# Norm chain moved to the end of the stage that makes the tokens, in a two-block transformer kernel on one core

## The chip, the core and the metric

One Trainium2 chip, one of its cores. The metric is the device time of one execution in microseconds, from the first to the last instruction of the program and what lies around it. All arithmetic is fp32 or, for the large products, pairs of fp32r parts.

## The reference

Two stacks of two layers each on 256 latent tokens of width 1024 (the first stack also carries 256 context tokens, so 512 in all, until its last mixer). Every layer is

```python
x = x + 0.5 * ffn(rms_norm(x, g1))          # SwiGLU, 1024 -> 2 x 2816 -> 1024
x = x + mixer(rms_norm(x, g2))              # attentions, a convolution, a product out
x = x + 0.5 * ffn(rms_norm(x, g3))

def rms_norm_2(x, g, eps=NORM_EPS):
    xf = x.astype(jnp.float32)
    y = xf * lax.rsqrt(jnp.mean(xf * xf, axis=-1, keepdims=True) + eps)
    return (y * g.astype(jnp.float32)).astype(x.dtype)
```

(in the first stack with a gate, a gain and a shift made from a conditioning vector). A last norm follows. That makes 13 norms: 5 on 512 tokens and 8 on 256.

## The kernel before, in words

Tokens are kept transposed: `k.x` is [128, 8, tokens], features on partitions in 8 chunks, tokens along the row. The program is a sequence of stages: `conditioning` (product `mod0`), then for each layer `half_ffn`, a mixer behind `norm_tokens`, `add_product_of_parts` (product `out`), `half_ffn`, and at the end `norm_tokens` and `ending`. Each stage is one or more `Block`s. Within a block each engine runs its own list of instructions in the order written, and a block ends when all engines have reached its end.

All weights come through a ring of 4 slots (`RING`), one unit of up to 128 x 2048 at a time, loaded by SP as PE finishes with a slot (`unit_done`). Before PE uses a unit it is split in two fp32r parts: ACT copies it to the high part (`split_high`, L472), then DVE subtracts to get the low part (`split_low`, L480). PE takes three matmuls for each product of parts (L496). Part buffers are 2 deep in stages on 512 tokens and in the mixers, 4 deep in `half_ffn` on 256 tokens.

The norm has two ends. Where a stage makes new tokens, ACT squares each chunk of `k.x` (L390) and POOL adds the squares of chunks 0 to 6 (L405); the last square stays apart. Where the next stage begins, PE sums both over the partitions with a matrix of ones (L418, L420), which leaves in PSUM the sum of squares of each token, equal on all 128 partitions; ACT takes the root of it (L967 or L513), DVE the reciprocal into `k.rinv` (L1053 or L537), and both of them go over 128 x tokens elements. `half_ffn` then scales chunk by chunk on DVE (L1060), shifts or copies on ACT to the high part `normed[0]` (L974, L976), and DVE makes the low part `normed[1]` (L1072, L1074); PE's first unit of the stage takes the chunks as they come. In `norm_tokens` the scaling is L544 or L541, and the block ends before the mixer's first matmul.

In `half_ffn`, ACT's list begins with the split of unit 0, the root, the split of unit 1, and then the 8 chunks; DVE's with the low part of unit 0, the reciprocal, then the chunks, then the low part of unit 1:

```python
            split_high(act, 0, 0)
...
            nc.scalar.activation(k.root[:, T], k.psum[:, 0, T], ACT.Sqrt, bias=k.eps[:, 0:1], scale=1.0 / D)\
                .then_inc(t["root_done"].sem, 1)
            split_high(act, 0, 1)
```

In `hybrid_mixer` (the mixer of the second stack) the norm's block splits unit 0 of the mixer's first product in the same way, so that `project_heads` begins with unit 0 ready. `conditioning` multiplies the conditioning vector with 9 units, places the results, and squares the opening tokens.

## Time and profile before

| | |
|---|---|
| time, median of 3 executions | 3957.33 us (3955.28 to 3962.86) |
| the profiled execution: its own time | 3963.74 us |
| its span, first to last instruction | 3961.7 us |
| PE busy with matmuls | 3490.9 us (88% of the span) |
| DVE, ACT, POOL busy | 2099.9 us (53%), 1412.2 us (36%), 229.1 us (6%) |
| mean granted TensorE clock | 0.933 of 2.4 GHz |

The profiled execution is 6.4 us longer than the median. A busy share is an average over all stages. For this change what counts is the stretch between one stage's last matmul and the next stage's first ones, 13 of them, and who is waited for there.

### The profile page before, as it was taken

The page shows a single profiled execution, that of the slowest core. Times are in us where ns is not written, and L with a number is a line of the kernel's source. Part 1 is how long each engine was busy: PE and PEld are TensorE (multiplying, and loading weights), DVE is VectorE, ACT ScalarE, POOL GpSimd, SP SyncE. Part 2 cuts the span into 40 slices and gives each one's busy share as a digit, 9 for nine tenths or more (in the row PEclk, how much of TensorE's full clock was granted, in tenths as well). Part 3 has the DMA queues.
Part 4 walks back from the last instruction along what each step waited for, and adds up shares of the span by engine and source line. Part 5 has one row for each costly group of instructions (what it writes and reads, how often), then busy time and mean ns, then how long its engine had stood idle before and what let it go on. Part 6 is the DMA issues. An engine that isn't in the chain of part 4 may idle for free. (4 is left out here: it accounts for less than half of the span.)

```text
span 3961.7 us, 54085 instructions
## 1 busy us (share of the span) xinstructions
PE 3490.9 (88%) x20506; PEld 2972.5 (75%) x20506; DVE 2099.9 (53%) x2729; ACT 1412.2 (36%) x2278; POOL 229.1 (6%) x169
## 2 busy tenths in 40 slices
PE   5999896789998999898799998769899999769898
PEld 4887642468887788664699998548899999548898
DVE  5767474547677433214454655554455545554554
ACT  3323302233333322212444544243344444243443
POOL 0000100100001000200000001200000001200000
PEclk8999898889999999998899999879999999879899
DMA  6666420016665233320166565204466564104464
GB/s 200 184 180 178 110 62 31 0 59 168 186 175 157 82 96 94 101 96 0 43 175 176 150 188 155 56 0 112 141 171 180 163 188 145 53 1 126 127 185 133
DMA packets 766417, 478.33 MB, mean 121 GB/s; under 512 B 35093, under 2 KB 743173, under 8 KB 766101
## 3 DMA queue, kind: packets, MB, share of 16 engines
q1 hardware_dynamic: 755872, 473.14, 42.2%
q10 hardware_dynamic: 10356, 2.63, 0.4%
q8 instruction: 126, 2.06, 0.2%
q14 instruction: 63, 0.51, 0.0%
HBM read 474.65 MB, written 1.05 MB: 120 GB/s over the span
## 5 line engine op out<-in xcount | busy, mean ns | idle before, releaser
L496 PE MATMUL psum<-normed,weights_part 128*128 128x256 f32 (+1 forms) x11232 | 1738.4, 317 | 86.7 <-DVE normed L1074 27.3
L496 PEld LDWEIGHTS psum<-normed,weights_part 128*128 128x128 f32 x11232 | 1586.7, 192 | 227.3 <-issue 82.1
L480 DVE TENSOR_TENSOR weights_part<-weights,weights_part 128x2048 fp32r<-128x2048 f32 (+1 forms) x397 | 847.4, 2137 | 755.3 <-ACT weights_part L472 755.1
L472 ACT ACTIVATE weights_part<-weights 128x2048 fp32r<-128x2048 f32 (+1 forms) x397 | 708.4, 1787 | 761.7 <-PE psum L496 350.1
L496 PE MATMUL psum<-hidden,weights_part 128*128 128x256 f32 (+1 forms) x4224 | 680.7, 323 | 0.0
L496 PEld LDWEIGHTS psum<-hidden,weights_part 128*128 128x128 f32 x4224 | 614.5, 190 | 61.5
L1267 DVE SCALAR_TENSOR_TENSOR stage<-weights,cond,stage 128x768 f32<-128x768 f32 x294 | 281.1, 1019 | 0.0
L405 POOL TENSOR_TENSOR square<-square,rinvs 128x256 f32<-128x256 f32 (+1 forms) x39 | 57.2, 1466 | 2490.3 <-ACT rinvs L390 2488.2
L1101 DVE SCALAR_TENSOR_TENSOR x<-psum,gate,x 128x256 f32<-128x256 f32 (+1 forms) x112 | 49.6, 479 | 130.8 <-PE psum L496 130.8
L858 DVE TENSOR_REDUCE negmax<-psum 128x1 f32<-128x256 f32 (+1 forms) x128 | 66.8, 524 | 94.7 <-PE psum L2347 20.0
L987 ACT ACTIVATE rinvs<-psum 128x256 f32<-128x256 f32 (+1 forms) x88 | 39.9, 453 | 212.9 <-PE psum L496 212.8
L1524 PE MATMUL psum<-h,weights 128*128 128x512 f32 (+1 forms) x224 | 98.8, 604 | 13.3 <-PEq L506 13.3
L989 ACT ACTIVATE hidden<-rinvs 128x256 f32 (+3 forms) x88 | 43.8, 498 | 177.1 <-DVE rinvs L1084 177.1
L989 ACT ACTIVATE hidden<-roots 128x256 f32 (+3 forms) x88 | 43.8, 498 | 176.2 <-DVE roots L1084 176.2
L987 ACT ACTIVATE roots<-psum 128x256 f32<-128x256 f32 (+1 forms) x88 | 40.1, 455 | 182.4 <-PE psum L496 182.2
L1084 DVE TENSOR_TENSOR rinvs<-rinvs,psum 128x256 f32<-128x256 f32 (+1 forms) x88 | 45.4, 516 | 100.2 <-ACT rinvs L987 100.2
L1524 PEld LDWEIGHTS psum<-h,weights 128*128 128x128 f32 (+1 forms) x224 | 42.1, 189 | 70.7 <-issue 70.7
L2339 PE MATMUL psum<-heads,stage 128*128 128x256 f32 (+1 forms) x128 | 49.0, 472 | 42.2 <-POOL stage L798 42.2
L496 PE MATMUL psum<-mixed_part,weights_part 128*128 128x512 f32 (+1 forms) x384 | 71.5, 351 | 11.4 <-DVE mixed_part L597 11.4
L1086 DVE TENSOR_TENSOR hidden<-rinvs,hidden 128x256 f32 (+3 forms) x88 | 46.3, 526 | 61.1 <-ACT hidden L989 61.1
L1086 DVE TENSOR_TENSOR hidden<-roots,hidden 128x256 f32 (+3 forms) x88 | 46.3, 526 | 60.7 <-ACT hidden L989 60.7
L1084 DVE TENSOR_TENSOR roots<-roots,psum 128x256 f32<-128x256 f32 (+1 forms) x88 | 45.4, 516 | 61.7 <-ACT roots L987 61.7
(304 smaller groups left out, 3234.7 us busy)
## 6 DMA issues: line engine op xcount, KB each, us to landing
weights<-in_l_ffn_w_in SPq DMA_DIRECT2D x176, 512.0 KB, 5.1
weights<-in_ffn_w_gu SPq DMA_DIRECT2D x176, 512.0 KB, 5.0
weights<-in_l_mod_w SPq DMA_DIRECT2D x168, 384.0 KB, 3.4
weights<-in_w_in SPq DMA_DIRECT2D x34, 1024.0 KB, 5.2
weights<-in_w_gate SPq DMA_DIRECT2D x64, 512.0 KB, 4.6
weights<-in_l_ffn_w_out SPq DMA_DIRECT2D x64, 384.0 KB, 3.9
weights<-in_ffn_w_down SPq DMA_DIRECT2D x64, 384.0 KB, 4.1
weights<-in_l_ffn_w_out SPq DMA_DIRECT2D x64, 320.0 KB, 3.2
```

The source lines that it names most:

```text
L405: k.nc.gpsimd.tensor_tensor(total, total, buffers[n % 2], ALU.add).then_inc(summed.sem, 1)
L472: nc.scalar.activation(k.parts[part][0][:, W], k.slots[slot][:, W], ACT.Copy).then_inc(high.sem, 1)
L480: nc.vector.tensor_tensor(k.parts[part][1][:, W], k.slots[slot][:, W], k.parts[part][0][:, W].bitcast(F32), ALU.subtract).then_inc(low.sem, 1)
L496: mm = k.nc.tensor.matmul(to, left[a], right[b], start=first and n == 0, stop=last and n == len(PASSES) - 1)
L858: nc.vector.tensor_reduce(k.negmax[:, j:j + 1], S[j], AX.X, ALU.max, negate=True).then_inc(t["maxed"].sem, 1)
L987: nc.scalar.activation(row[:, T], k.psum[:, bank(spec, c), T], ACT.Silu).then_inc(t["silu_done"].sem, 1)
L989: nc.scalar.activation(one(k.hidden[0], i * RING + c, col=T), row[:, T], ACT.Copy)\
L1084: nc.vector.tensor_tensor(row, row, k.psum[:, bank(spec, c) + 1, T], ALU.mult).then_inc(t["gated"].sem, 1)
L1086: nc.vector.tensor_tensor(one(k.hidden[1], i * RING + c, col=T), row, one(k.hidden[0], i * RING + c, col=T).bitcast(F32), ALU.subtract)\
L1101: last = nc.vector.scalar_tensor_tensor(row, k.psum[:, bank(spec, c), part], gate(chunk, cond) if callable(gate) else gate, row, ALU.mult, ...
L1267: ins = k.nc.vector.scalar_tensor_tensor(total, self.buffer(n), scale, total, ALU.mult, ALU.add)
L1524: mm = nc.tensor.matmul(k.psum[0:m, 2 * slot + t, :], lhs, k.h[:, kc, :], start=kc == 0, stop=kc == KD - 1)
```

## The change

The sum, root and reciprocal of the norm leave the start of the consuming stage and go to the end of the producing one, in a new function `invert_rms` that closes `conditioning`, `add_product_of_parts` and `half_ffn`. They are formed with tokens on partitions: the squares are the stationary operand and a single column of ones streams past them, so that each block of 128 tokens gives one column, [128, 4] for 512 tokens and [128, 2] for 256. ACT takes the root and DVE the reciprocal of these few columns. PE then spreads them back over all partitions, by one matmul per block of tokens with the inverse column, repeated along its row, as stationary operand and the identity streaming past. The result `k.spread` stays in a PSUM bank and DVE's scaling reads it there.

Part buffers now live at fixed places for the whole program, are dealt out to units beforehand (`deal_parts`), and have one count of splits for all stages. This lets a stage split units of the next one (`ahead`). That is used in three places: `conditioning` splits unit 0 of the first `half_ffn`, and the product `out` of the second stack finds its first two units split, as before. Everywhere else `ahead` is 0. In `half_ffn` the split of unit 0 still comes first; that of unit 1 now stands behind the 8 chunks on ACT too. In `hybrid_mixer` unit 0 is no longer split in the norm's block but at the start of `project_heads`. `conditioning` also loads ACT's table with the root ahead of its squares.

```diff
-def sum_over_chunks(k, pe, tokens):
+def invert_rms(k, block, tokens, last, bank=None):
...
+    blocks = [(b, slice(b * P, (b + 1) * P)) for b in range(tokens // P)]
+    sums = k.psum[:, 2 * ((last + 2) % RING) + 1, 0:len(blocks)]
+    k.spread = k.psum[:, 2 * (last % RING) + 1 if bank is None else bank, 0:tokens]
+    root, inverse = k.rms[:, 0, 0:len(blocks)], k.rms[:, 1, 0:len(blocks)]
+    chunks_squared, chunks_summed = squared.base + KD, summed.base + KD - 2
+
+    @block.tensor
+    def _(pe):
+        pe.wait_ge(summed.sem, chunks_summed)
+        pe.wait_ge(k.banks_free, RING + last)
+        for n, part in enumerate((total, buffers[(KD - 1) % 2])):
+            if n:
+                pe.wait_ge(squared.sem, chunks_squared)
+            for b, columns in blocks:
+                mm = k.nc.tensor.matmul(sums[:, b:b + 1], part[:, columns], k.const("ones")[:, 0:1],
+                                        start=(n, b) == (0, 0), stop=n == 1, skip_group_check=True)
+        mm.then_inc(t["added"].sem, 1)
+        pe.wait_ge(t["inverse"].sem, t["inverse"].base + 1)
+        for b, columns in blocks:
+            mm = k.nc.tensor.matmul(k.spread[:, columns], inverse[:, b:b + 1].broadcast_to([P, P]), k.const("ident"),
+                                    start=True, stop=True)
+        mm.then_inc(t["spread"].sem, 1)
+
+    @block.scalar
+    def _(act):
+        act.wait_ge(t["added"].sem, t["added"].base + 1)
+        k.nc.scalar.activation(root, sums, ACT.Sqrt, bias=k.eps[:, 0:1], scale=1.0 / D).then_inc(t["root"].sem, 1)
+
+    @block.vector
+    def _(dve):
+        dve.wait_ge(t["root"].sem, t["root"].base + 1)
+        k.nc.vector.reciprocal(inverse, root).then_inc(t["inverse"].sem, 1)
...
         def _(act):
-            split_high(act, 0, 0)
-
-            act.wait_ge(t["summed"].sem, t["summed"].base + 1)
-            nc.scalar.activation(k.root[:, T], k.psum[:, 0, T], ACT.Sqrt, bias=k.eps[:, 0:1], scale=1.0 / D)\
-                .then_inc(t["root_done"].sem, 1)
-            split_high(act, 0, 1)
+            for q in range(ready, 1):
+                split(split_high, act, 0, q)
             for c in range(KD):
                 act.wait_ge(t["scaled"].sem, t["scaled"].base + c + 1)
...
-            for q in range(2, depth):
-                split_high(act, 0, q)
+            for q in range(max(ready, 1), depth):
+                split(split_high, act, 0, q)
...
-            split_low(dve, 0, 0)
-            dve.wait_ge(t["root_done"].sem, t["root_done"].base + 1)
-            nc.vector.reciprocal(k.rinv[:, T], k.root[:, T]).then_inc(t["inverse_done"].sem, 1)
-            dve.wait_ge(t["inverse_done"].sem, t["inverse_done"].base + 1)
+            for q in range(ready, 1):
+                split(split_low, dve, 0, q)
...
                 for cond, part in parts_of_tokens:
                     last = nc.vector.scalar_tensor_tensor(k.rows[c % 2][:, part], k.x[:, c, part], gain(c, cond),
-                                                          k.rinv[:, part], ALU.mult, ALU.mult)
+                                                          k.spread[:, part], ALU.mult, ALU.mult)
...
-            each_unit(act, 0, RING, lambda i, c: split_high(act, i, c))
-            each_unit(act, RING, spec.n, lambda i, c: split_high(act, i, c), False)
-            if l == 0:
-                for c in range(KD):
-                    square_chunk(k, act, TOK, c)
+            for c in range(spec.n + 1):
+                split_high(k, act, 0, spec.start + c)
+            prepare_sqrt(k)
+            for c in range(KD):
+                square_chunk(k, act, TOK, c)
...
         @block.scalar
         def _(act):
-            split_high(act, 0, 1)
+            for c in range(ready, 2):
+                split(split_high, act, c)
```

ACT at the last `half_ffn` that follows a product `out` (the end of the one, the branches to the next block, the start of the other). Before; L390 is the last square, L472 the split of a unit, L967 the root, L974 the copy of a chunk to its high part:

```order
L390 ACTIVATE rinvs<-x 128x256
L560 UNCONDITIONAL_BRANCH
L962 UNCONDITIONAL_BRANCH
L472 ACTIVATE weights_part_1_26<-weights 128x2048
L967 ACTIVATE roots<-psum,eps 128x256
L472 ACTIVATE weights_part_2_26<-weights 128x2048
L974 ACTIVATE normed_26<-roots 128x256
L974 ACTIVATE normed_26<-rinvs 128x256
```

and the change, from the same square on to the end of the chunks:

```order
L393 ACTIVATE rinvs<-x 128x256
L444 UNCONDITIONAL_BRANCH
L447 ACTIVATE rms<-psum,eps 128x2
L582 UNCONDITIONAL_BRANCH
L996 UNCONDITIONAL_BRANCH
L513 ACTIVATE weights_part_1_1_51<-weights 128x2048
L1004 ACTIVATE normed_23_30583<-roots 128x256
...
L1004 ACTIVATE normed_23_30583<-rinvs 128x256
L513 ACTIVATE weights_part_0_1_49<-weights 128x2048
L513 ACTIVATE weights_part_2_1_53<-weights 128x2048
```

The root went ahead of the block's end and covers 2 columns; the split of unit 1 went from ahead of the 8 chunks to behind them.

DVE at the same place, before (L1053 is the reciprocal, L1060 the scaling):

```order
L1049 UNCONDITIONAL_BRANCH
L480 TENSOR_TENSOR weights_part_1_26<-weights,weights_part_1_26 128x2048
L1053 RECIPROCAL rinvs<-roots 128x256
L1060 SCALAR_TENSOR_TENSOR roots<-x,vec,rinvs 128x256
L1060 SCALAR_TENSOR_TENSOR rinvs<-x,vec,rinvs 128x256
```

and the change:

```order
L452 RECIPROCAL rms<-rms 128x2
L582 UNCONDITIONAL_BRANCH
L1077 UNCONDITIONAL_BRANCH
L521 TENSOR_TENSOR weights_part_1_1_52<-weights,weights_part_1_1_51 128x2048
L1086 SCALAR_TENSOR_TENSOR roots<-x,vec,psum 128x256
L1086 SCALAR_TENSOR_TENSOR rinvs<-x,vec,psum 128x256
```

The reciprocal went ahead of the block's end; the low part of unit 0 stays between it and the scaling, which reads PSUM.

PE there, in the change (before, the two matmuls L418 and L420 stood behind the second branch):

```order
L427 UNCONDITIONAL_BRANCH
L435 MATMUL psum<-consts,square 128x1 x2
L435 MATMUL psum<-consts,rinvs 128x1 x2
L440 MATMUL psum<-consts,rms 128x128 x2
L582 UNCONDITIONAL_BRANCH
L1037 UNCONDITIONAL_BRANCH
L535 MATMUL psum<-normed_23_30583,weights_part_1_1_51 128x256
```

Two wide matmuls became four of one column and, behind ACT and DVE, two of 128.

## Rows read from the trace of the kernel before

**Rows 1.** A stretch of half_ffn: PE, PEld, DVE, ACT, POOL busy; clock; DMA share; GB/s.

```profile
2192.00:2377.00 185.00, 184.53 (x1538) 184.33 (x1537) 98.13 (x96) 82.74 (x90) 7.85 (x6) 1.00 0.64 181
```

**Rows 2.** Timeline (start, length in us) from a product out to half_ffn, 256 tokens.

```profile
3745.53 0.72 POOL L405 TENSOR_TENSOR square<-square 128x256 f32<-128x256 f32 x1 [3.90 <-ACT square L390]
...
3746.63 1.91 ACT L472 ACTIVATE weights_part<-weights 128x2048 fp32r<-128x2048 f32 x1 [0.88 <-PEq L560]
...
3750.78 1.75 DVE L1053 RECIPROCAL rinvs<-roots 128x256 f32<-128x256 f32 x1
3752.56 0.49 DVE L1060 SCALAR_TENSOR_TENSOR roots<-x,vec,rinvs 128x256 f32<-128x256 f32 x1
...
3759.12 3.70 ACT L472 ACTIVATE weights_part<-weights 128x2048 fp32r<-128x2048 f32 x2
...
3761.93 13.26 PEld L496 LDWEIGHTS psum<-normed,weights_part 128*128 128x128 f32 x110 [0.24 <-DVE weights_part L480]
```

**Rows 3.** Timeline from layer 0's product out to half_ffn, 512 tokens.

```profile
872.85 1.26 POOL L405 TENSOR_TENSOR square<-square 128x512 f32<-128x512 f32 x1 [8.15 <-ACT square L390]
...
882.02 0.88 DVE L1060 SCALAR_TENSOR_TENSOR roots<-x,gain,rinvs 128x256 f32<-128x256 f32 x2
...
894.26 0.91 ACT L976 ACTIVATE normed<-rinvs,mod 128x256 fp32r<-128x256 f32 x2 [0.80 <-DVE rinvs L1060]
...
898.94 0.60 ACT L987 ACTIVATE roots<-psum 128x512 f32<-128x512 f32 x1 [2.47 <-PE psum L496]
```

**Rows 4.** Timeline from conditioning to the first half_ffn; DMA issues there, us to landing.

```profile
59.26 11.90 SPq L332 DMA_DIRECT2D weights<-in_l_ffn_w_in  x8
...
61.77 0.61 ACT L390 ACTIVATE square<-x 128x512 f32<-128x512 f32 x1
...
71.17 1.26 POOL L405 TENSOR_TENSOR square<-square 128x512 f32<-128x512 f32 x1
...
80.68 0.88 DVE L1060 SCALAR_TENSOR_TENSOR roots<-x,gain,rinvs 128x256 f32<-128x256 f32 x2
...
weights<-in_l_ffn_w_in SPq DMA_DIRECT2D x8, 512.0 KB, 6.0
```

**Rows 5.** Timeline from half_ffn to a mixer of the second stack, 256 tokens.

```profile
2377.39 0.42 DVE L1101 SCALAR_TENSOR_TENSOR x<-psum,x 128x256 f32<-128x256 f32 x1 [3.53 <-PE psum L496]
...
2384.54 3.26 DVE L541 SCALAR_TENSOR_TENSOR heads<-x,vec,rinvs 128x256 f32<-128x256 f32 x8
```

**Rows 6.** Timeline from half_ffn to layer 0's mixer, 512 tokens.

```profile
475.49 0.88 DVE L1101 SCALAR_TENSOR_TENSOR x<-psum,gate,x 128x256 f32<-128x256 f32 x2 [6.61 <-PE psum L496]
...
484.59 4.91 DVE L544 TENSOR_TENSOR h<-x,rinvs 128x512 f32<-128x512 f32 x8
```

**Rows 7.** Timeline from the last half_ffn to the last norm, 256 tokens.

```profile
3946.70 0.42 DVE L1101 SCALAR_TENSOR_TENSOR x<-psum,x 128x256 f32<-128x256 f32 x1 [3.53 <-PE psum L496]
...
3951.31 2.07 DVE L541 SCALAR_TENSOR_TENSOR h<-x,vec,rinvs 128x256 f32<-128x256 f32 x5
```

**Rows 8.** Small operations: timeline of conditioning, groups by shape, and a stretch at the end.

```profile
51.47 0.60 PE L1383 MATMUL psum<-consts,roots 2*128 2x2 f32 x4 [0.17 <-DVE roots L1414]
...
L425 ACT ACT_TABLE_LOAD x12 | 15.4, 1283 | 0.2
...
L425 ACT ACTIVATE spare<-eps 128x1 f32<-128x1 f32 x12 | 2.4, 203 | 0.1
...
L866 DVE RECIPROCAL inverse<-rowsum 128x4 f32<-128x4 f32 x32 | 5.4, 168 | 0.0
...
3954.80:3958.60 3.80, 3.65 (x16) 3.27 (x16) 2.11 (x4) 0.00 (x0) 0.00 (x0) 0.50 0.21 81
```

**Rows 9.** A group by shape on DVE with an operand in PSUM; busy us, mean ns.

```profile
L1101 DVE SCALAR_TENSOR_TENSOR x<-psum,gate,x 128x256 f32<-128x256 f32 x88 | 38.8, 478 | 103.9 <-PE psum L496 103.9
```

**Rows 10.** The granted clock (after POOL's column) in two stretches between stages.

```profile
72.00:83.00 11.00, 3.75 (x4) 1.17 (x4) 7.78 (x8) 7.08 (x8) 0.44 (x1) 0.50 0.74 235
874.00:877.00 3.00, 2.55 (x3) 1.18 (x4) 0.57 (x1) 1.91 (x1) 0.11 (x1) 0.50 1.01 256
```

More of the change, by code:

```diff
@@ L497, in product_of_parts, with norm_tokens @@
     return mm
-def norm_tokens(k, tokens, gain, shift=None, dst=None, parts=None, splits=None):
+def norm_tokens(k, tokens, gain, shift=None, dst=None, parts=None):
     x, dst = k.x, k.h if dst is None else dst
-    mean, root, scaled, high = (k.tally(n) for n in ("mean_done", "root_done", "scaled", "normed_high"))
+    scaled, high = k.tally("scaled"), k.tally("normed_high")
     T = slice(0, tokens)
@@ L548, in _, with add_product_of_parts @@
                     k.nc.vector.tensor_tensor(parts[1][:, c, T], dst[:, c, T], parts[0][:, c, T].bitcast(F32), ALU.subtract)
-    for t, n in ((mean, 1), (root, 1), (scaled, 1 + KD), (high, KD if parts is not None else 0)):
+    for t, n in ((scaled, KD), (high, KD if parts is not None else 0)):
         t.close(n)
-def add_product_of_parts(k, spec, tokens, source, parts, gate=None, splits=None, before=0):
+def add_product_of_parts(k, spec, tokens, source, parts, gate=None, ahead=0, bank=None):
     nc, T = k.nc, slice(0, tokens)
     high, low = k.tally("source_high"), k.tally("source_low")
-    split_high, split_low, wait_parts = splits or weight_parts(k, [spec], 2)
-    ready = 0 if splits is None else 2
+    ready, after = k.ahead[spec.name], k.next_spec(spec)
+    k.ahead[after.name] = ahead
     with nc.Block() as block:
@@ L946, in looped, with split @@
         return stream is None and s < len(specs) - 1
-    split_high, split_low, wait_parts = weight_parts(k, specs, depth, RING if stream is None else STREAM_PAIRS)
-    with ffn_buffers(k, tokens, depth), nc.Block() as block:
+    def split(half, engine, i, q):
+        if q < total + ahead:
+            half(k, engine, i, first + q)
+    ffn_buffers(k, tokens, depth)
+    with nc.Block() as block:
         total_units = k.plan[-1].start + k.plan[-1].n
@@ L1916, with project_heads @@
 SCALED_UNITS = (0, 1, 4, 8, 10)
[L1919 removed]
+def project_heads(k, l):
     nc, spec = k.nc, k.spec(f"in_b{l}")
@@ L1925, in project_heads, with split @@
     values = [k.va[:, :, 0:256], k.va[:, :, 256:512], k.bv, k.cv, k.dv]
-    split_high, split_low, wait_parts = splits
+    ready = k.ahead[spec.name]
+    def split(half, engine, c):
+        if c < spec.n:
+            half(k, engine, 0, spec.start + c)
     with nc.Block() as block:
@@ L2265, in merge_branches, with split @@
     parts = [[(0, 16, y["a"]), (3, 20, y["d"])], [(1, 16, y["b"]), (2, 18, y["c"])]]
-    split_high, split_low, wait_parts = splits
+    def split(half, engine, i, c):
+        half(k, engine, i, spec.start + c)
     def all_units(engine, unit):
@@ L2416, in second_block @@
+    sb = region(k, PARTS_2 + 27 * 1024)
+    k.merged = sb("merged", [P, KD, LAT], F32)
+    merged_parts = [sb(f"merged_part{n}", [P, KD, LAT], F32R) for n in range(2)]
+    out = k.spec(f"out_b{l}")
+    merge_branches(k, l)
+    k.ahead[out.name] = 2
+    add_product_of_parts(k, out, LAT, k.merged, merged_parts)
 def second_block(k, w):
```

357 lines of the change are left out of this document (171 added, 186 removed).

## The prediction

> **What bounds the kernel now.** I read the page first (the table above): PE is busy for 88% of the span, DVE for half of it. Then the busy times by stretch, to see what a delay between stages costs. Within `half_ffn` on 256 tokens PE works 184.5 of 185 us at the full clock [rows 1]; the other stages of that kind and those on 512 tokens show the same. The DMA queues are busy there too (share 0.64), but PE never starves. So such a stage starts late by x and ends late by x. What PE stands still for lies between the stages, and there I read timelines, which show the order of releases.
>
> At the change from a product out to `half_ffn` on 256 tokens [rows 2], POOL's last add ends at 3746.25 (3745.53 + 0.72). The block ends 0.38 later, at 3746.63. ACT splits unit 0 (1.9), DVE makes its low part, and at 3750.78 the reciprocal starts, 1.75 long; scaling starts at 3752.56. PE's sum and ACT's root lie beside the splits and are waited for by nobody. So 6.31 us pass from the last add to the scaling: 0.38 of block end, 4.15 of splits, 1.75 of reciprocal. The first unit then takes chunks as DVE makes them, and PE's weight loads go on at 3761.93, just after the low part of unit 1 ("0.24 <-DVE weights_part L480"): PE waits for that part too.
>
> **What is removed, added and moved.** Removed from the path is a reciprocal of 1.75 us (256 tokens) or 3.35 (512, same view). Added ahead of the block's end is a serial chain: products with one column, root, reciprocal, spread. It used to lie beside the splits and now lies ahead of them. Moved behind the chunks is ACT's split of unit 1.
>
> *Price of the chain.* No row has these shapes. The nearest are two small products that take 0.60 us at the full clock (4 records; an fp32 product is two), and 8 products of 128 columns, 16 records, that take 3.65 at half clock [rows 8]. I take, for 2, 4 and 8 products, 0.6, 1.05 and 1.95 us at full clock and 0.9, 1.8 and 3.65 at half. The root is like the one-column one, 0.20; the reciprocal like that of 128x4, 0.17 [rows 8]; three hand-overs together 0.25. Lower bound: the one-column products at half of this; upper: every product like the 0.45 a piece at half clock.
>
> *Product out to `half_ffn`, 256 tokens, three times.* After the last add: start 0.05, 4 products 1.05, root, reciprocal and hand-overs 0.62, spread 0.75 (clock on the edge), block end 0.38, so 2.85; then the splits, 4.15: 7.0 against 6.3. **+0.7 each, +2.1.**
>
> *The same on 512 tokens, once.* POOL ends at 874.11 and scaling starts at 882.02, 7.91 later [rows 3]. The clock is at half from 874 [rows 10], since PE has stood still. 0.05 + 3.65 + 0.62 + 1.8 + 0.38 = 6.5, and 4.15: 10.65. **+2.7** (+0.4 at the full clock).
>
> *Conditioning.* Here unit 0 is split ahead, which saves 4.15 at the start of the stage, but its split stands in ACT's list before the squares. Its two DMAs are issued from 59.26 on and take 6.0 us to land [rows 4], so they are there at about 66.2; the split ends at 68.1, table load and root for it (1.28 and 0.20, [rows 8]) at 69.6. The squares start there and not at 61.77, 7.8 later. Before, POOL ended 10.7 after the first square, at 72.43, with a first add twice as long as the others (I take one us off): now at 79.3. The chain at half clock (0.50 from 72 to 83, [rows 10]) takes 6.5: scaling at 85.8 against 80.68. **+5.1** (+2.7 at the full clock).
>
> *`half_ffn` to what follows.* There POOL is long done and the last chunk of x is the last input. Its add ends at 2377.81, scaling starts at 2384.54 [rows 5]: 6.7. Now: square 0.45, 2 products 0.6, 0.62, spread 0.6, block end 0.38: 2.65. Towards another `half_ffn` (once, and once over the block with the rotary tables) the splits bring this to 6.8: **0**. Towards the mixers of the second stack 4.1 us are gained in the norm's block, but unit 0 is then split at the start of `project_heads`, where PE used to start at once: 4.15 given back. **+0.1**, twice. Towards the last norm, 4.19 before [rows 7]: **-1.5**. On 512 tokens: square 0.65, 4 products 1.05, 0.62, spread 1.8, block end 0.38: 4.5. Towards layer 0's mixer it was 8.2 [rows 6]: **-3.7**; towards layer 1's it was 7.1 by the same view, and the clock is still full there (spread 1.05, so 3.75): **-3.3**; towards `half_ffn`, once, 8.65 against 8.54 by the same view, **+0.1**. The norm's block on 512 tokens begins the mixer with nothing split, so these two gains stay.
>
> *The second unit.* ACT has finished the 8 chunks at 3759.12 and goes on with the splits of units 2 and 3; the low part of unit 1 is done at 3761.9. Now the split of unit 1 stands at 3759.12 (in the old clock): high part done at 3761.0, low part (2.3) at 3763.35, PE 1.45 us later than before. What hid this split was the reciprocal, which is gone. DVE stands behind it with the low parts of units 2 and 3, each needed a unit later. Five stages: **+7.3.** On 512 tokens ACT's chunks end at 895.17, so the low part comes at 899.4, while PE finished its first unit at 898.9 [rows 3]; with the other two, where it finished sooner, I take 0.9 each: **+2.7.**
>
> *Nothing more.* DVE now reads the row from PSUM. With an operand in PSUM the same instruction takes 478 ns over 256 elements [rows 9], with the row in SBUF 490 [rows 2]; I price it at 0. The Trainium skill, VectorE: DVE Perf Modes, section on the TRN2 errata, gives a fixed cost of 120 cycles with a source in PSUM against 58 in SBUF, which would be 65 ns for each scaling and 19 in place of 12 us for the whole change; these rows disagree with it. The table load before the root at the first and at the seventh norm lay beside a low part and is worth nothing. SP's and POOL's lists are the same.
>
> Sum: 2.1 + 2.7 + 5.1 + 0.2 - 1.5 - 3.7 - 3.3 + 0.1 + 7.3 + 2.7 = **+11.7 us**, so 3975.4 for the profiled execution of 3963.74. That one is 6.4 above the median of the runs shown; against the median, 3957.3, the forecast is **3969 us**, slower by 0.3%. A measurement of this kernel tells 0.2% (8 us) from no change.
>
> **Rivals.** (a) *The second unit costs nothing*, because PE is held up on unit 0 anyway. Against: PE's wait in [rows 2] names DVE's low part. If it holds, 10.0 of the sum fall away: 3959, no change. Close to it is (b) *DMA absorbs what PE loses* in the 256-token stages: ACT does wait for weights there. It would take 7.3 + 2.1 off: 3960. Against: PE's 184.5 of 185.
>
> (c) *The clock stays full in the chain.* The added products come where PE stood still. If only the chain is spared, 2.4 at conditioning, 2.3 at layer 0's product out, 0.7 at layer 0's mixer: +6, 3963, no change. If PE is kept at the full clock over the whole change of stages, the first units are spared as well: two mixers of the second stack start at half clock for about 5.4 us and lose 2.6 each, the two of the first stack some 4 in all; with further 0.7 together -16: **3953**, on the other side. It is decided by whether the clock drops between the column products and the first unit. Against: it drops in every such stretch, with two wide products in it, and the chunks start no sooner. The Trainium skill, TensorE: Matmul & The Clock Gate, section on what happens, has the half clock as the default that only activity lifts; by that rule, with which [rows 10] agree, a few short products don't.
>
> (d) *The row in PSUM slows the scaling*, or the chain is dearer. Forms of this instruction spread by 70 ns (420 to 490); over the 112 scalings that stand on the path this is 7.8 us: 3977. At the chain's upper bound it is 8 more as well.
>
> (e) *The gains in the mixers are not kept*, since something else (a load, POOL's clearing) is waited for: 3976. Little for it: PE's first matmul stands at once behind the block's end.
>
> **Chances.** The forecast as it stands, +8 to +17: 0.50. (a) and (b): 0.14. (c) chain only: 0.11, all of it: 0.07. (d), (e): 0.13. The rest, 0.05, on either side. Faster by over 0.2% takes the whole of (c) and more: 0.08. Within 0.2%: 0.28, from (a), (b), both of (c) in part, and the low edge of the forecast. Slower: 0.64. The range goes from (c)'s full form and (a), about 3956, to (d), 3980.
>
> **What would show it.** In the timeline of the changed kernel: between the last add of POOL and the block's end 2.5 us in place of 0.4 at the 256-token products out; scaling of the last `half_ffn` 7.0 after that add; ACT's split of unit 1 directly behind the last chunk, and PE's second unit about 10.8 after the first scaling in place of 9.4; squares of conditioning from 69.6 on; the mixers of the first stack 3 to 4 us nearer to the stage before, those of the second in place. The forecast is wrong if PE does not wait for the second unit, if the column products take clearly less than 0.25 us each, or if the granted clock at the first units is 1.0.

## The result, and the profile after

The changed kernel takes **3987.40 us** (median of 4 executions, 3984.68 to 3989.12) against 3957.73 of the kernel before on the same chip: 1.0077 times, 95% interval 1.0063 to 1.0091. The direction was forecast, the size was not: +29.7 us where I had +11.7, and outside the range. The profiled execution took 3987.76 us, its span is 3985.8 us, 24.1 over the span before. One execution of e8 below took 5150 us at a mean clock of 0.639 and is left out of its median.

From the page after the change, the busy times and the group of the products with `normed` (busy us, mean ns; idle time ahead of them and what ended most of it):

```profile
PE 3516.0 (88%) x20670; PEld 3006.3 (75%) x20670; DVE 2071.1 (52%) x2729; ACT 1408.2 (35%) x2278; POOL 227.9 (6%) x169
...
L535 PE MATMUL psum<-normed,weights_part 128*128 128x256 f32 (+1 forms) x11232 | 1746.3, 318 | 98.3 <-DVE weights_part L521 43.4
```

The same group in the page of before:

```profile
L496 PE MATMUL psum<-normed,weights_part 128*128 128x256 f32 (+1 forms) x11232 | 1738.4, 317 | 86.7 <-DVE normed L1074 27.3
```

DVE is busy 29 us less (the reciprocals). PE is busy 25 us more: its 20670 records are 164 more than before, all of them the chain's, but their busy time is only 12 us more than that of the two wide products that they replace. The rest is products that take longer. In this group PE now waits 43.4 us for the low parts of weights, where the largest sum of waits for one operation was 27.3 before.

The timeline from the last product out to `half_ffn` (start, length; it answers to [rows 2]):

```profile
3766.37 0.72 POOL L408 TENSOR_TENSOR square<-square 128x256 f32<-128x256 f32 x1 [3.94 <-ACT square L393]
...
3767.14 0.61 PE L435 MATMUL psum<-consts,square 128*128 128x1 f32 x4 [2.09 <-POOL square L408]
...
3767.61 0.58 PE L435 MATMUL psum<-consts,rinvs 128*128 128x1 f32 x4
3768.23 0.26 ACT L447 ACTIVATE rms<-psum,eps 128x2 f32<-128x2 f32 x1 [1.64 <-PE psum L435]
3768.53 0.17 DVE L452 RECIPROCAL rms<-rms 128x2 f32<-128x2 f32 x1 [2.69 <-ACT rms L447]
...
3768.75 1.22 PE L440 MATMUL psum<-consts,rms 128*128 128x128 f32 x4 [0.55 <-DVE rms L452]
3770.33 1.91 ACT L513 ACTIVATE weights_part<-weights 128x2048 fp32r<-128x2048 f32 x1 [1.83 <-PEq L582]
...
3774.48 0.47 DVE L1086 SCALAR_TENSOR_TENSOR roots<-x,vec,psum 128x256 f32<-128x256 f32 x1
...
3776.01 7.27 PE L535 MATMUL psum<-normed,weights_part 128*128 128x256 f32 x48 [6.03 <-DVE normed L1098]
...
3780.99 5.50 ACT L513 ACTIVATE weights_part<-weights 128x2048 fp32r<-128x2048 f32 x3
...
3785.28 2.98 PE L535 MATMUL psum<-normed,weights_part 128*128 128x256 f32 x14 [2.00 <-DVE weights_part L521]
```

The chain stands where the forecast had it: 3.24 us from POOL's last add (3767.09) to the block's end (3770.33; 2.85 forecast, the spread takes 1.22 and not 0.75), 4.15 of splits, and the scaling. The second unit starts 10.80 after the first scaling (forecast 10.8), and PE has stood for 2.00 us ahead of it. What the forecast did not have is in a row of windows over 3.4 us of that unit, and of the same unit of the first `half_ffn` of the second stack (after POOL's column: the granted clock, DMA share, GB/s):

```profile
3785.80:3789.20 3.40, 3.40 (x18) 3.40 (x18) 3.40 (x2) 2.36 (x3) 0.00 (x0) 0.51 0.79 224
2205.40:2208.80 3.40, 3.40 (x18) 3.40 (x17) 3.40 (x2) 2.09 (x3) 0.00 (x0) 0.50 0.73 206
```

PE, started, fed and then stopped, falls to 1.2 GHz again at two of the five starts, and loses 1.7 us more at each of the two. The conditioning (answers to [rows 4]):

```profile
69.21 0.61 ACT L393 ACTIVATE square<-x 128x512 f32<-128x512 f32 x1
...
78.77 1.86 PE L435 MATMUL psum<-consts,square 128*128 128x1 f32 x8 [7.10 <-POOL square L408]
...
82.91 2.08 PE L440 MATMUL psum<-consts,rms 128*128 128x128 f32 x8 [0.57 <-DVE rms L452]
...
85.32 0.87 DVE L1086 SCALAR_TENSOR_TENSOR roots<-x,gain,psum 128x256 f32<-128x256 f32 x2 [2.47 <-PEq L1386]
```

The whole span, stretch by stretch, from the same instructions in both timelines (last add to x, first scaling, first product; rounded; us by which the changed kernel falls further behind):

| stretch | forecast | first trace |
|---|---|---|
| conditioning, to the first scaling | +5.1 | +4.6 |
| in the three `half_ffn` of 512 (second unit) | 3 x 0.9 | +0.6, +0.6, +0.9 |
| in the five `half_ffn` of 256 (second unit) | 5 x 1.45 | +1.4, +3.6, +1.3, +1.5, +3.8 |
| to layer 0's mixer, to layer 1's | -3.7, -3.3 | -4.4, -2.1 |
| products out to `half_ffn`: 512, then 256 | +2.7, 3 x 0.7 | +2.9, +1.5, +0.8, +1.1 |
| `half_ffn` to `half_ffn` 512, over the tables, 256 | +0.1, 0, 0 | +0.4, +0.5, -0.1 |
| to the two hybrid mixers (first product), to the last norm | +0.1, +0.1, -1.5 | +0.1, +0.1, -1.5 |
| **inside the four mixers** | **0** | **+2.7, +0.8, +2.8, +0.4** |

The rows sum to +3.9 for the changes of stage (forecast +1.7), +13.7 for the second units (+10.0) and +6.7 inside mixers (0). So about half of the surprise is where I had looked for nothing. In a hybrid mixer (the last two of the four) PE runs full for 100 us at the full clock, and more slowly than before. A stretch of 80 us of its projection, before and then after:

```profile
2400.00:2480.00 80.00, 80.00 (x682) 80.00 (x681) 42.88 (x40) 37.34 (x41) 1.31 (x1) 1.00 0.59 176
```

```profile
2415.00:2495.00 80.00, 80.00 (x669) 80.00 (x669) 42.88 (x40) 35.83 (x41) 0.00 (x0) 1.00 0.57 175
```

682 matmuls against 669 in the same time, both at clock 1.00. From start to start a matmul takes 0.1178 us before and 0.1200 after (the last five units of the second mixer's projection 0.1133 and 0.1200), in every record. A projection unit is 0.11 us longer, a merge unit 0.18, which by 16 units each is 4.6 us in the first mixer, and 5.7 in the second, where five units lose 0.32. These two figures are worked out from the rates; the mixers as a whole grew by 2.8 and 0.4 us in this trace. The rest came back elsewhere in them, and I did not find where. None of PE's instructions there had been changed. What had been changed is where tensors lie.

### The profile page after: what moved, and what is told of

Same layout as the page of the kernel before. It is cut to its first block and busy times, and to the rows that moved or that the text cites. A ratio compares the mean times of both kernels' runs of the same rounds, so it can differ in the third digit from the quotient of the medians.

```text
span 3985.8 us, 54430 instructions
## 1 busy us (share of the span) xinstructions
PE 3516.0 (88%) x20670; PEld 3006.3 (75%) x20670; DVE 2071.1 (52%) x2729; ACT 1408.2 (35%) x2278; POOL 227.9 (6%) x169
## 5 line engine op out<-in xcount | busy, mean ns | idle before, releaser
L535 PE MATMUL psum<-normed,weights_part 128*128 128x256 f32 (+1 forms) x11232 | 1746.3, 318 | 98.3 <-DVE weights_part L521 43.4
L535 PEld LDWEIGHTS psum<-mixed_part,weights_part 128*128 128x128 f32 x384 | 62.9, 202 | 20.0 <-DVE weights_part L521 11.8
```

The lines of the kernel that those rows point to most:

```text
L535: mm = k.nc.tensor.matmul(to, left[a], right[b], start=first and n == 0, stop=last and n == len(PASSES) - 1)
```

## The experiments

Twelve kernels, timed in turns with the kernel before on their chip. "Changed" is the kernel after the change.

**e1. The second unit's high part ahead of the chunks.**

```
-            for q in range(ready, 1):
+            for q in range(ready, 2):
                 split(split_high, act, 0, q)
 ...
-            for q in range(max(ready, 1), depth):
+            for q in range(max(ready, 2), depth):
                 split(split_high, act, 0, q)
```

> The changed kernel with one thing undone: in half_ffn ScalarE forms the high part of the second weight unit ahead of the eight chunks of the tokens, as before the change; VectorE's order stays. Theory A (the second unit that comes late is the largest part of the loss: in the trace of the changed kernel TensorE stands 0.7 to 2.0 us ahead of the second unit at five starts, and at two of them the granted clock falls to half again for 3.4 us): TensorE has no stop ahead of the second unit, the second fall of the clock is gone, and the time falls by 10 to 14 us, to 3974 to 3978. Theory B (the stop only moves a wait that the high half of the third and fourth unit then gives back): the time falls by less than 4 us.

Measured: 3975.86 us, 1.0054 (1.0040 to 1.0068), 11.5 us under the changed kernel by medians, 9 by ratios. The same place as above, in its timeline:

```profile
3770.70 3.70 ACT L513 ACTIVATE weights_part<-weights 128x2048 fp32r<-128x2048 f32 x2
...
3773.50 4.70 PE L535 MATMUL psum<-normed,weights_part 128*128 128x256 f32 x37 [0.18 <-DVE weights_part L521]
```

PE's stop is 0.18 us and not 2.00 (before the change 0.04). The five `half_ffn` of 256 tokens take 193.3, 193.6, 192.9, 192.9 and 196.7 us from first product to last addition (changed 194.8, 196.5, 194.3, 194.3, 196.8; before 193.4, 192.9, 193.0, 192.9, 193.0). Theory A holds, though by ratios the gain is just under its 10 us. The last of the five stayed long for another cause: near its end PE stood 2.1 us waiting for DVE's low part of `hidden`, and the clock was at half for 3.4 us after it.

**e2. The first unit split ahead of every stage.** `ahead=1` at the products out and at 512 tokens, `ahead=2` at the four ends of `half_ffn` of 256 tokens that have a stage behind them with parts, and the second high part behind the root:

```
         k.nc.scalar.activation(root, sums, ACT.Sqrt, ...).then_inc(t["root"].sem, 1)
+        if high is not None:
+            split_high(k, act, 0, high)
```

> The changed kernel with the first weight unit of each half_ffn and of each hybrid mixer split while the stage ahead of it still multiplies (two units where the tokens are 256 and a half_ffn comes before), and the second unit's high part behind the root in the chain elsewhere. Theory A (the split of the first unit, 1.9 us on ScalarE and 2.3 us on VectorE, is what stands between the end of the chain and the scaling in the changed kernel): scaling starts within 0.5 us of the end of the spread at seven half_ffn starts and the first product of the two hybrid mixers comes 4 us nearer, 9 x 4.2 = 38 us, and the second unit's stops go as well, 13 us: 3935 to 3945, under both kernels. Rival (the splits that stand ahead of the last squares on ScalarE and of the last additions on VectorE make the end of the product late by the 2 to 4 us that they take, at every boundary): 3965 or more.

Measured: 3959.38 us, 1.0012 (1.0003 to 1.0021): 26 to 28 us gained, not 42 to 52. The time lies between the two theories, and each held in its place. Behind a product out the scaling starts 3.5 to 4.0 us after POOL's last add and not 7.1 to 7.8. At the ends of `half_ffn` the rival's mechanism is in the timeline:

```profile
2370.53 1.91 ACT L516 ACTIVATE weights_part<-weights 128x2048 fp32r<-128x2048 f32 x1 [2.97 <-DMA weights<-in_w_in]
2372.34 0.40 ACT L393 ACTIVATE rinvs<-x 128x256 f32<-128x256 f32 x1
2372.47 2.29 DVE L524 TENSOR_TENSOR weights_part<-weights,weights_part 128x2048 fp32r<-128x2048 f32 x1 [2.56 <-ACT weights_part L516]
...
2374.68 0.75 DVE L1140 SCALAR_TENSOR_TENSOR x<-psum,x 128x256 f32<-128x256 f32 x2
```

ACT holds the next stage's split in hand and waits for its weights; the square stands behind it, and on DVE the two last additions behind the low part. These four `half_ffn` take 194.9 to 196.7 us, the last, with nothing behind it, 194.3 (before 192.9 to 193.4). From last addition to scaling it takes 4.1 to 4.95 us at the three in the second stack, where 2.7 do towards a mixer.

**e3. Operands moved by a few bytes.**

```
+SHIFTS = {"ffn2_0": 192, "ffn1_1": 64, "ffn2_1": 192, "ffn1_b0": 64, "mix_b0": 192, ...}
-    sb = region(k, PARTS_2 if depth == 2 else PARTS_4)
+    sb = region(k, (PARTS_2 if depth == 2 else PARTS_4) + shift)
```

> The changed kernel with the tokens' operands of TensorE (normed, and in a half_ffn hidden) moved in SBUF by a small, different number of bytes in each stage: 192 in both second half_ffn of the first stack, 64 in the second layer's first one, and in the second stack 64, 192, 32, 96, 64, 128 bytes stage by stage. Nothing else changes. Theory A (the time from one matmul of 256 columns to the next depends on how the two operands lie to each other: it was 0.1178 us in the hybrid mixer's projection before, where they lay an odd multiple of 64 bytes apart, and is 0.1200 us in the changed kernel, where they lie a multiple of 1024 bytes apart): with 192 bytes the projection runs at 0.118 us, the half_ffn at 256 columns too (0.1200 in both kernels so far), and the time falls by 5 to 20 us. Theory B (the pace comes from something else, the order or number of the instructions or what the other engines read): every matmul keeps 0.120 us, and the time stays within 4 us of the changed kernel.

Measured: 3973.96 us (one execution), 13.8 under the changed kernel's profiled one. The first hybrid mixer's projection, 192 bytes on (the window's columns as above), has 709 matmuls in 80 us, 0.1133 each:

```profile
2410.00:2490.00 80.00, 80.00 (x709) 80.00 (x708) 44.45 (x41) 38.76 (x42) 0.00 (x0) 1.00 0.61 184
```

At 512 columns the same 192 bytes cost: 0.2333 us and not 0.2267. Theory A holds: the place sets the rate; its "multiple of 1024" was too coarse (below).

**e4. The squares of the conditioning early**, all eight behind the fourth split.

```
             for c in range(spec.n + 1):
+                if c == RING:
+                    for n in range(KD):
+                        square_chunk(k, act, TOK, n)
                 split_high(k, act, 0, spec.start + c)
             prepare_sqrt(k)
-            for c in range(KD):
-                square_chunk(k, act, TOK, c)
```

> The changed kernel with ScalarE squaring the eight chunks of x behind the fourth split of the conditioning, where it waits for weights from 39.5 to 46.9 us, and no more behind the last split. Theory A (the chain at the end of the conditioning is late by the eight squares and seven additions that start only at 69.2 us): the column products start when the last unit is placed, at 72.1 us and not 78.8, and the time falls by 6 us, to 3981. Rival (the splits of units 4 to 8 come later by the squares, and with them the last product): the time falls by less than 2 us.

Measured: 3984.53 us, 1.0078 (1.0064 to 1.0091): nothing by ratios, 2.9 us by medians, and neither is clear of the uncertainty. The timeline speaks for the rival. From the fourth on each square waits for POOL's add of 1.26 us, ACT comes back to its splits only after the eighth, and the splits of three units stand in a row behind:

```profile
48.83 0.63 ACT L393 ACTIVATE square<-x 128x512 f32<-128x512 f32 x1 [0.79 <-POOL square L408]
50.27 0.63 ACT L393 ACTIVATE rinvs<-x 128x512 f32<-128x512 f32 x1 [0.81 <-POOL square L408]
50.80 5.57 ACT L513 ACTIVATE weights_part<-weights 128x2048 fp32r<-128x2048 f32 x3
```

The last unit of the conditioning is multiplied 6 us later; scaling starts at 82.78, 2.5 earlier than in the changed kernel. With the squares in the gaps (five, one, two), in e8 to e11, it starts at 76.0 to 78.1.

**e5. The distance alone, in the kernel before.** Before, `normed` starts 16384 + 4096 + 6144 + 192 + 1024 + 50176 = 78016 bytes ahead of the parts in the projection and 27840 in the merge. Seen from the parts, `normed` lies at 64 modulo 256 in both. The 192 bytes are set out ahead of `normed`, the parts stay where they are, and the distances become 77824 and 27648, multiples of 1024 as in the changed kernel (the expectation has them 1024 too short):

```
+        k.best, k.index_weight = sb("best", [P, 2, 8]), sb("index_weight", [P, 16])
+        k.lam_exp, k.minus_lam = sb("lam_exp", [P, 2]), sb("minus_lam", [P, 1])
         k.normed = [sb(f"normed{n}", [P, KD, LAT], F32R) for n in range(2)]
 ...
-        k.best, k.index_weight = sb("best", [P, 2, 8]), sb("index_weight", [P, 16])
-        k.lam_exp, k.minus_lam, k.forget = sb("lam_exp", [P, 2]), sb("minus_lam", [P, 1]), sb("forget", [4, LAT])
+        k.forget = sb("forget", [4, LAT])
```

> The kernel before with four small tensors of the hybrid mixers (192 bytes in a partition) set out ahead of the two normed tensors and not behind them, so that normed and the parts of the weights lie 76800 bytes apart in the projection and 26624 in the merge, multiples of 1024, where they lay 78016 and 27840 apart, 192 over one; no instruction changes. Theory A (the distance of the two operands sets the time from one matmul to the next, and the change lost about 10 us of TensorE in the two hybrid mixers by it): the projections go from 0.1178 (0.1133 in the last units of the second) to 0.1200 us a matmul, each unit of them is longer by 0.11 to 0.32 us and each of the merge by 0.18, 4.7 us in the first mixer and 5.6 in the second, and the time rises by 8 to 11 us, to 3963 to 3966. Theory B (something else in the changed kernel slows these matmuls): the pace stays, and the time within 3 us.

Measured: 3966.79 us against 3958.08, +8.7, ratio 1.0022 (1.0012 to 1.0032). The window of the projection gives the changed kernel's count:

```profile
2400.00:2480.00 80.00, 80.00 (x669) 80.00 (x668) 42.89 (x40) 35.81 (x41) 0.74 (x1) 1.00 0.58 175
```

Theory A. In its one trace the hybrid mixers are 3.1 and 0.5 us longer, as in the changed kernel's (2.8, 0.4), and layer 0's mixer 2.8 us with no edit there at all. Single traces show less than the medians do: the two hybrid mixers together take 940.3 to 941.8 us in the six traces with distance 0 throughout (changed, e1, e2, e4, e5, e12), 937.5 before and 934.6 in e9, which has the distance of before. So the price is 8.7 us by ten executions against fifteen, 3 to 7 by traces.

e5 also tells the distance from a place. The parts of the projection did not move, and their products went from 0.1178 to 0.1200. And in the kernel before, `normed` starts at the same place in `half_ffn` (0.1200) and in the projection (0.1178). So neither operand's address by itself gives the rate.

**e6. More distances**, by e3's edit.

```
+SHIFTS = {"ffn1_0": 128, "ffn2_0": 256, "ffn1_1": 320, "ffn2_1": 224, "ffn1_b0": 256, "mix_b0": 320, "ffn2_b0": 384,
+          "ffn1_b1": 512, "mix_b1": 448, "ffn2_b1": 832}
```

> The changed kernel with the operands of the tokens moved by further numbers of bytes, one for each stage, to see which give what pace: 128, 256 and 320 at 512 columns; 224, 256, 320, 384, 512, 448 and 832 at 256 columns. Theory A (only the distance modulo 1024 counts, and a distance that is a multiple of 256 is as slow as 0): 256, 384 and 512 keep 0.120 us at 256 columns, 320, 448 and 832 give 0.113 to 0.118. Theory B (any distance off zero is quick): all seven give 0.118 or less. At 512 columns, where 192 bytes gave 0.2333 us, 64 gave 0.2290 and 0 gave 0.2267, nothing is expected to be quicker than 0.2267.

Measured: 3980.31 us (one execution). What e3, e6 and the others show, by the distance from the parts to the tokens' operand modulo 256 bytes, us from start to start of a matmul, mean over a stretch at full clock:

| modulo 256 | 256 columns | 512 columns |
|---|---|---|
| 0 (0, 256, 512 bytes) | 0.1200 | 0.2267 |
| 32 | 0.1177, 0.1167 | |
| 64 (64, 320, 832; the hybrid mixers before) | 0.1178; in the last five units of a projection, where tokens and parts change roles, 0.1133 or 0.1178 (the first mixer before and in e9) | 0.2289 |
| 96 | 0.1200 | |
| 128 (128, 384) | 0.1187 to 0.1199 | 0.2318, in some units 0.2333 |
| 192 (192, 448) | 0.1133, in some stages 0.1178 | 0.2333 |
| 224 | 0.1183 | |

Theory A, with 256 for 1024: 256 and 512 bytes are as slow as 0 at 256 columns, and at 512 columns 0 and 256 are the best.

**e7. 192 bytes in every stage of 256 tokens**, by e3's edit, and in the products out:

```
+SHIFTS = {"ffn2_1": 192, "ffn1_b0": 192, "mix_b0": 192, "ffn2_b0": 192, "ffn1_b1": 192, "mix_b1": 192, "ffn2_b1": 192}
-    sb = region(k, PARTS_2 + 27 * 1024)
+    sb = region(k, PARTS_2 + 27 * 1024 + 192)
-            sb = region(k, PARTS_2)
+            sb = region(k, PARTS_2 + (192 if tokens == LAT else 0))
```

> The changed kernel with the tokens' operands 192 bytes further on in every stage of 256 tokens (half_ffn, hybrid mixers, the products out), nothing else. Theory A (this distance gives 0.1133 us a matmul where the changed kernel takes 0.1200, as the look at it showed in two stages, and TensorE bounds all these stages): five half_ffn with 1584 products each, two mixers with 1328 and three products out with 192 gain 0.0067 us each, 11150 x 0.0067 = 74 us, to about 3913. Rival (TensorE's next limit there is the split or the loads, so that a shorter pace only makes it wait): less than 40 us, above 3947.

Measured: 3934.31 us, 0.9943 (0.9928 to 0.9958), 53 under the changed kernel: between the two. In the profiled execution, of some 210 units of 256 columns outside the merges about two thirds ran at 0.1133 us a matmul and one third at 0.1178. Summed over the intervals between their starts that is 50 us less than at 0.1200, and 5 more in the merges (0.0034 us in each of 32 x 48): 55, where the spans differ by 53.8 and the medians by 53. So nothing new holds TensorE up. The step that A had wrong is that one distance gives one rate.

**e8. All three:** e2's and e7's edits, and the squares in ACT's gaps:

```
+            squares = {RING: range(0, 5), RING + 1: range(5, 6), spec.n: range(6, KD)}
             for c in range(spec.n + 1):
+                for n in squares.get(c, ()):
+                    square_chunk(k, act, TOK, n)
                 split_high(k, act, 0, spec.start + c)
```

> The kernel of the run with the units split ahead, with the tokens' operands 192 bytes further on in every stage of 256 tokens, and with the squares of the conditioning in the gaps where ScalarE waits for weights (five behind the fourth split, one behind the fifth, two behind the ninth). Theory A (the three are independent): 28 us by the units ahead, 74 us by the pace and 4 us by the squares off 3987, about 3881. Rival (at a quicker pace the splits come late again and the gains don't add): 3900 or more.

Measured: 3898.7 us, 0.9851 (0.9833 to 0.9869): 89 us of the 106 that A added up, and 1 us under the rival's bound. What is missing is not lost between the edits. A had 74 us for the distance, and e7, not yet measured then, gave 53; with that the sum is 28 + 53 + 4 = 85, so the three do add. From last addition to scaling it takes 4.95 us at the ends of `half_ffn`, as in e2.

**e9. Three things put right, the chain left as the change made it:** e1's edit, e8's squares, and

```
+SHIFTS = {"mix_b0": 64, "mix_b1": 64}
```

> The changed kernel with three things put right and the rest of the change kept (the chain in its new form at the end of the stage before, the first unit's split behind the block): the second unit's high part ahead of the chunks, normed 64 bytes further on in the two hybrid mixers, which is the distance modulo 256 of the kernel before, and the squares of the conditioning in ScalarE's gaps. Theory A (these three places hold nearly all of the loss): 10 us by the second unit, 9 us by the distance and 7 us by the squares off the changed kernel's 0.8 per cent over the kernel before, 29.7 - 26 = 4 us over it, ratio 1.000 to 1.002. Rival (a loss is left that no run has named, in the chain or the first units): 10 us or more over the kernel before, 1.0025 or more.

Measured: 3961.63 us, 1.0011 (1.0003 to 1.0020), 4.8 us over the kernel before. Theory A: the three hold 25 (by medians) to 26 (by ratios) of the 30 us. By the edit of the squares the first scaling stands 9.3 us before the changed kernel's and 4.7 before that of the kernel before, so that edit does more than undo its part.

**e10. 448 bytes** for 192 in e8, and in the conditioning

```
-        invert_rms(k, block, TOK, spec.start + spec.n - 1, 7)
+        invert_rms(k, block, TOK, spec.start + spec.n - 1, 7, highs_after(k, spec, 1))
```

which names the unit whose high part stands behind the root.

> The kernel of the run with all three edits, with 448 bytes in place of 192 in the stages of 256 tokens, and in the conditioning the high part of the second unit behind the root as well. Theory A (the distance counts modulo 256, and the stages at 0.1178 us a matmul there, four of some seventeen, took that pace by chance of the moment): the same paces, 0.1133 and 0.1178, in other stages perhaps, and the time within 5 us of that run's, 0.984 to 0.987 of the kernel before. Rival (448 is a distance of its own): a pace of 0.120 or more in some stage, 10 us or more longer.

Measured: 3894.49 us, 0.9840 (0.9825 to 0.9855). Theory A: its full-size products show no rate but 0.1133 and 0.1178. Of the 27 stretches with one operand of the tokens (three products out, four in each `half_ffn`, two in each projection) 7 ran at 0.1178 in e8's trace and 10 in this one, four of them the same.

**e11. One unit ahead, later**, in e10. In the ends of `half_ffn` of 256 tokens:

```
                        square_chunk(k, act, tokens, c)
+                       if ahead and at(spec, c) == total - 3:
+                           split_high(k, act, 0, first + total)
```

and the low part behind the addition of the same chunk on DVE.

> The kernel of the run with all edits at 448 bytes, with one unit split ahead at the ends of the half_ffn of 256 tokens in place of two, behind the square of the last chunk but two and not ahead of that of the last but three, and the second unit's high part behind the root in the chain there too. Theory A (in the run with the units ahead ScalarE stood at those ends with the next stage's first split in hand, waiting 3.5 and 2.5 us for its weights, and the squares and VectorE's additions stood behind it: from the last addition to the scaling 4.95 us, where 2.7 do, and 1.3 to 3.3 us more in the stage, five times): from the last addition to the scaling 2.7 to 3.0 us, the stage 1 to 3 us shorter, in all 15 to 20 us: 3875 to 3880, 0.980 of the kernel before. Rival (the split then comes so late that the last addition waits for its low part): no gain or a loss, 3890 or more.

Measured: **3877.30 us, 0.9794 (0.9780 to 0.9808)**: 110 us under the changed kernel, 82 under the one before and 17 under e10. Theory A. The same end as in e2's rows, now with the chain on its own products and nothing ahead of the last addition:

```profile
2338.54 0.42 DVE L1150 SCALAR_TENSOR_TENSOR x<-psum,x 128x256 f32<-128x256 f32 x1 [1.43 <-PE psum L538]
2339.00 0.42 ACT L393 ACTIVATE rinvs<-x 128x256 f32<-128x256 f32 x1 [1.44 <-DVE x L1150]
...
2341.67 3.22 DVE L566 SCALAR_TENSOR_TENSOR heads<-x,vec,psum 128x256 f32<-128x256 f32 x8 [1.10 <-PEq L1005]
```

2.70 us from last addition to scaling here; the five `half_ffn` take 184 to 189 us. Not all of the gain is the edit's. From last addition to scaling the four ends give 7.5 us against e10's trace, but 0.1178 also occurs in only 5 of the 27 stretches where e10's had 10, and by the intervals that is 8 us.

**e12. The changed kernel again**, with no edit.

> The changed kernel as it is, once more, to see what of its first trace is a matter of the execution. Theory A (order and place decide): 0.7 to 0.8 per cent over the kernel before; the matmuls of 256 columns take 0.1200 us in all stages; from the first product of a half_ffn to its second unit the same stops. The share that is the clock's (2.7 us more than before inside layer 0's mixer, falls to half in the second unit at two starts) may lie elsewhere. Rival (the pace is drawn anew at each execution): another pace in some stage.

Measured: 3987.74 us, 1.0076 (1.0064 to 1.0088); every stage of 256 columns at 0.1200. Layer 0's mixer is again 2.9 us longer than before. The clock's share moved: no fall in the unit at 2205 and none at the last start, but one each at the two starts between, the first hybrid mixer 4.2 us shorter than in the first trace and the second 5.1 longer, at the same rate of PE.

## Why the prediction was wrong, step by step

**What bounds the kernel** held: a delay between stages came out at the end. But I read from it only that a stage's start moves its end, and not that a stage in which PE works 184.5 of 185 us is as long as its matmuls: the rate of PE was part of the bound.

**The step that failed is "Nothing more".** I listed what the diff does to instructions and left out what it does to addresses. The parts moved into a fixed region, and the hybrid mixers' operands from 64 to 0 modulo 256 bytes. The term was absent, and measures 8.7 us alone (e5; 4.8 to 12.7 by its interval), about half of the 18 us by which the forecast missed. The row that could have warned stood in the trace of before: 256-column matmuls at 0.1178 in the mixers and at 0.1200 in `half_ffn`, at one clock.

**The second unit** was right in mechanism and time of arrival (10.80) and mis-sized: +13.7 us in the trace where I had 10.0. I priced the wait; at two starts the wait also cost the clock. e1 gives 9 to 11.5 back, near the forecast, so how much the term was short is known from traces alone. Rival (a) falls with it, and (b): no stage absorbed its late start.

**The chain** was 0.4 us dearer behind products out of 256 tokens (0.8 to 1.5 lost for the forecast 0.7), by the spread at half clock. At 512 tokens, +2.9 for 2.7; conditioning +4.6 for 5.1, squares from 69.21 for 69.6. `half_ffn` to what follows came within 0.5 us, but for the first stack's mixers. There I had the clock the wrong way round: half at layer 0's and full at layer 1's. The spread of these two chains:

```profile
483.92 1.16 PE L440 MATMUL psum<-consts,rms 128*128 128x128 f32 x8 [0.57 <-DVE rms L452]
```

```profile
1663.78 2.08 PE L440 MATMUL psum<-consts,rms 128*128 128x128 f32 x8 [0.57 <-DVE rms L452]
```

So layer 0's gained 4.4 for the forecast 3.7, and layer 1's 2.1 for 3.3.

**What e9 leaves.** It keeps only the chain and the first units' splits, whose forecast terms sum to -3.4 without the conditioning, and its first scaling stands 4.7 before that of the kernel before (76.00 and 80.68): 8.1 us less was due, and 3.0 less came by the spans of the traces, 4.8 more by medians. Of the 5 us that the traces lack, 4.4 have a place: its changes of stage sum to -3.7 and not -8.1, with 2.4 of it at the three products out of 256 tokens (1.3 to 1.7 lost each for 0.7) and 1.4 at the first stack's mixers, where it gained 3.2 and 2.3. From scaling to last addition the `half_ffn` are 2.5 us longer together than before, the mixers 1.7 shorter. The other 8 us, between traces and medians, are mostly that the traced execution of the kernel before, 3963.7 us, lay 6 to 7 us over that kernel's medians.

**The scaling with the row in PSUM** takes 0.47 to 0.48 us, with the row in SBUF it took 0.49 [rows 2]: rival (d)'s first half is out, and the Trainium skill's higher fixed cost for PSUM (VectorE: DVE Perf Modes, TRN2 errata) does not show in these rows either. **(c), a clock that stays full,** is out as a whole: the clock was 0.59 on average from 70 to 81 us, and 0.930 over the whole after 0.933. It came true in one place, the 0.7 us at layer 0's mixer (1.00 from 481 to 485). The page that I named for it (the Trainium skill, TensorE: Matmul & The Clock Gate, What's actually happening) has the low clock as the default; the 0.59 there agrees. **(e)** fell at layer 0; a third of the gain is missing at layer 1, but by the half clock in the chain and not by a wait for something else.

**The subtraction of 6.4 us** was a step of its own. Before's executions spread from 3948.6 to 3966.9 over all calls, and its profiled one lay high; those of the changed kernel lie within 3984.7 to 3989.1 in ten. Against traces the miss is 24.1 - 11.7 = 12.4 us; the other 5.6 of it is this. Layer 0's mixer belongs here: 2.7 and 2.9 us longer in the changed kernel, but 2.8 in e5 too, which there is the kernel before, instruction for instruction: before's first trace was lucky in its clock. The fourteen traces show two lengths of this mixer: 387.5 to 387.9 us with the clock at half for 86 us of it (before, e6, e10), and 390.2 to 390.4 us with 95 us at half (the other eleven). Both occur with the changed code, so this is no cost of the change. Which executions get which falls stays open.

## What to carry to other kernels

Where an engine is full, compare its rate per instruction across stages before pricing anything else; the same matmul at two rates at one clock means that something outside the instruction sets it, and a change that moves buffers moves it too. A step taken from ahead of a chain to behind it must be followed one unit further than the first: price the wait, and look whether the clock falls in it. Splits done ahead pay only where their input has landed and nobody's last step stands behind them: two units early gave 26 to 28 us, and one unit placed later 17 more, about half of it by the edit itself.

## What the runs showed of the hardware

The time of a matmul from SBUF at full clock depended on how its two operands' addresses lie to each other modulo 256 bytes: 0.1133 to 0.1200 us at 256 columns, 0.2267 to 0.2333 at 512, and the best distance for the one (192) is the worst for the other. At 64 and at 192 bytes two rates occur, 0.1133 and 0.1178, the same code in the same place taking one or the other in different kernels (e7, e8, e10). What draws between them, and why the distance counts, no run here shows. In the changed kernel's two traces, the stop behind the first 48 matmuls of the five `half_ffn` of 256 tokens was 0.74 to 2.00 us long. The four stops of 1.85 to 2.00 us were each followed by 3.4 us at 1.2 GHz, the six of 0.74 to 1.65 us by none. The low part came at the same time after the scaling each time (10.8 us; 11.3 behind layer 1's product out).
